# Short convolution, its silu, its product and its root moved to later picks of the gather loop

## The chip, the cores and the metric

The kernel runs on one core of one Trainium2 chip. The metric is the device time of one execution in microseconds (us), as the median of several runs; less is better. "PE" is the matrix engine, "DVE" the vector engine, "ACT" the scalar engine, "POOL" the GpSimd engine and "SP" the sync engine.

## The reference

One layer of a streaming encoder for 1024 frames of width 1024. First comes token mixing, then an expert layer in which every frame fetches 128 pairs of rows from two tables of 16384 experts:

```python
proj = jnp.einsum('bsd,dc->bsc', rms_norm(h, norm_mix_gain), w_in)
p_in, q_raw, k_raw, v_raw, z, b_raw, a_raw = jnp.split(proj, SPLIT_POINTS, axis=-1)
pool_out = multiscale_pool_mixer(p_in, w_pool, b_pool, pool_scale)
qkv = silu(causal_depthwise_conv(concat(q_raw, k_raw, v_raw), conv_w))   # 4 taps
q, k = l2_normalize(q) * HEAD_DIM ** -0.5, l2_normalize(k)
o = gated_delta_rule_chunked(q, k, v, g, beta)                            # 4 heads, chunks of 64
h = h + concat(pool_out, rms_norm(o, o_gain) * silu(z)) @ w_out
# expert layer, for blocks of 128 frames
q = h_t @ w_query                    # 8 heads x 2 halves
s1, s2 = q[:, :, 0] @ sub_keys_1, q[:, :, 1] @ sub_keys_2
experts, gates = top 16 of the sums of the two top 16's, softmax
act = gelu(h_t . expert_u[experts])
h = h + sum over (gates * act) * expert_v[experts]
out = rms_norm(h, norm_final_gain)
```

## The kernel before, in words

**The gather loop.** The frames are worked on in 8 tiles of 128. A tile has 8 retrieval heads with 16 picks each, so 128 picks, and the loop has 1024. At each pick POOL issues one indirect transfer (L806) that brings one row of both expert tables for each of the 128 frames, 1 MB, into one of 8 places of a ring. DVE multiplies and sums the row with the frame (L1504, "the dot"). ACT takes the gelu of the sum (L1107), scales a small diagonal with it (L1111) and makes the next diagonal (L1099). After every odd pick PE adds two picks with 16 matmuls (L1845 and L1846, "the pair"; in the last tile L1829). Only when the pair of an old pick is done may POOL issue the transfer that overwrites its place, eight picks later. In the text 3/3.7 is pick 7 of head 3 of tile 3, tiles, heads and picks being counted from 0.

**What else runs in the loop.** Everything else is laid beside the picks by a hand-written order. Each engine has its own loop over the picks and at each pick does the pick's own work first and then what is due: the search for the next heads' picks on DVE (`search`), the delta rule of the next tile as 35 steps for each of two pairs of heads (`delta`, begun at picks 13 and 45 of a tile, so that its steps 3 to 18 lie on heads 1 and 3), the scores of a later head on PE (L1760, picks 12 and 13), the norms. On ACT step 5 of the delta rule is the copy L926 and steps 6, 9, 12 and so on the copy L929; PE's products of these steps are L1537.

**The units.** The input projection of the later frames is cut into 38 units of 128 output columns by 256 frames, one unit in each head from 0/5 on. A unit w is worked on by the functions called `unit`, over two heads. In its own head PE projects it in two halves (L1691, 8 matmuls each in the trace), ACT copies it out of the accumulator at pick 11 (L1061 to L1065), and DVE makes the four taps of its convolution (L1439 and three times L1441) at picks 12 to 15. In the next head ACT takes the silu (L1039) and, for the query and key units, the square (L1042); PE sums the squares by one product (L1670); ACT takes the root (L1047); DVE makes the reciprocal (L1416) and the product (L1419) at picks 8 and 9; at pick 11 the result is stored. There are 16 query and key units ("q"), 8 value units ("v", no square and no root), 8 pooling units and 6 gate units. Whether the weights of a unit are loaded late is told by `load_late`.

**Order on an engine.** Instructions of an engine start in the order in which they stand. ACT does the pick (L1107, L1111, L1099), then `unit`, then `delta`; PE does `delta`, then the pair, then `unit`, then the scores; DVE does the dot, the search, `delta`, then `unit`.

## Time and profile before

| what | value |
|---|---|
| median of 3 runs | 2986.09 us (2985.65 to 2986.99) |
| the profiled execution, its own time | 2982.09 us |
| its span, first to last instruction | 2979.9 us |
| busy: PE, DVE, ACT, POOL | 78%, 73%, 50%, 42% |
| granted clock of PE, mean | 0.913 of 2.4 GHz |
| first and last gather issued | 258.6 us, 2953.4 us |

The profile is of one execution. Its own time is the span and 2.2 us around it. In the timelines each row has the start and the length of an instruction or of a few merged ones, and in brackets how long the engine had been idle before it and what it waited for. The length of a merged row goes from the start of the first to the end of the last.

### The profile page before, as it was taken

Reading aid. Unit: us, or ns where it says so; the run is one execution under the profiler, and the core shown is the slowest. Engines: PE = TensorE matmul, PEld = TensorE weight load, DVE = VectorE, ACT = ScalarE, POOL = GpSimd, SP = SyncE. Lnnn points to the kernel's source line nnn. Section 1 sums busy time; section 2 is a strip of 40 time slices with the busy share of each in tenths; the row PEclk is TensorE's granted clock in tenths of the full one; section 3 lists DMA queues with packets and bytes.
Section 4 is the critical chain, followed back from the end, with each engine's and each line's share of the span. In section 5 each row is a group of like instructions: output and inputs, shape, how many; then the busy total and the mean of one; then the engine's idle time right before and its main releaser. Section 6 shows DMA issues by size and latency. Waiting matters only on the chain.

```text
span 2979.9 us, 38619 instructions
## 1 busy us (share of the span) xinstructions
PE 2329.6 (78%) x12696; PEld 1126.5 (38%) x12696; DVE 2185.6 (73%) x5443; ACT 1484.0 (50%) x4204; POOL 1240.4 (42%) x1168
## 2 busy tenths in 40 slices
PE   7998778778886778677786778767786778778887
PEld 6454444234432444233442344324431333223332
DVE  2756776788877886778887887678876787776664
ACT  3623455565654554444655654544453454444444
POOL 1002444444444444443444344444444444544442
PEclk9999899889898999898998889889997888989999
DMA  4435999999999999999999999999999999999998
GB/s 169 151 112 220 408 419 413 421 421 407 408 420 421 418 418 419 419 416 408 404 420 421 407 420 415 420 418 419 404 415 421 418 411 415 404 416 420 421 421 345
DMA packets 194009, 1157.77 MB, mean 389 GB/s; under 512 B 20880, under 2 KB 48912, under 8 KB 62224
## 3 DMA queue, kind: packets, MB, share of 16 engines
q0 software_dynamic: 147456, 1073.81, 87.1%
q1 hardware_dynamic: 29392, 55.54, 5.2%
q10 hardware_dynamic: 16960, 25.96, 2.3%
q8 instruction: 101, 1.65, 0.2%
q14 instruction: 100, 0.82, 0.1%
HBM read 1139.49 MB, written 15.73 MB: 388 GB/s over the span
## 4 chain that ended last, share of the span: by engine, by line
DMA 41%; PE 26%; DVE 10%; ACT 9%; issue 4%; POOL 3%; ACTq 0%; DVEq 0%; POOLq 0%
DMA ring_mem<-in_experts,work 41%; PE bank L1845 11%; DVE ring_mem L1504 6%; POOL ring_mem L806 3%; PE bank L1713 3%; PE bank L1829 3%; PE bank L1537 3%; PE bank L1760 2%; ACT work L1111 2%; ACT L1107 1%; ACT work L1107 1%; ACT L984 1%; ACT work L1099 1%; PE bank L1691 1%; PE bank L1638 1%
## 5 line engine op out<-in xcount | busy, mean ns | idle before, releaser
L806 POOL DMA_INDIRECT ring_mem<-in_experts,work x1024 | 1174.9, 1147 | 1464.9 <-PE bank L1846 1145.8
L1504 DVE CUSTOM_DVE_ANT_0 ring_mem<-ring_mem,work 128x1024 f32<-128x1024 f32 x1024 | 1251.9, 1223 | 557.3 <-DMA ring_mem<-in_experts,work 553.4
L1845 PE MATMUL bank<-ring_mem,work 64*64 64x512 f32 x3584 | 1016.3, 687 | 356.5 <-ACT work L1111 356.3
L1846 PE MATMUL bank<-ring_mem,work 64*64 64x512 f32 x3584 | 1016.3, 687 | 0.0
L1107 ACT ACTIVATE work<-work 128x1 f32<-128x1 f32 x1024 | 206.0, 201 | 1197.3 <-DVE work L1504 1192.3
L1845 PEld LDWEIGHTS bank<-ring_mem,work 64*64 64x64 f32 x3584 | 247.8, 147 | 854.7 <-ACT work L1111 504.1
L1111 ACT ACTIVATE work<-work 128x64 f32<-128x64 f32 (+1 forms) x1024 | 364.0, 355 | 34.1 <-ACT work L1107 0.2
L1099 ACT ACTIVATE work<-kept,work 128x64 f32<-128x64 f32 x896 | 298.4, 333 | 10.9 <-DVE work L1377 10.9
L1829 PE MATMUL bank<-ring_mem,work 128*128 128x512 f32 x512 | 248.8, 621 | 47.1 <-ACT work L1111 46.7
L1537 PE MATMUL bank<-work 128*128 128x128 f32 x1080 | 190.5, 316 | 117.9 <-ACT work L929 54.9
L1760 PE MATMUL bank<-late,work 128*128 128x256 f32 x1008 | 253.9, 396 | 9.8 <-ACT late L964 7.5
L1537 PEld LDWEIGHTS bank<-work 128*128 128x128 f32 x1080 | 155.8, 213 | 249.9 <-ACT work L929 82.5
L1846 PEld LDWEIGHTS bank<-ring_mem,work 64*64 64x64 f32 x3584 | 248.0, 147 | 0.0
L1760 PEld LDWEIGHTS bank<-late,work 128*128 128x128 f32 x1008 | 188.4, 195 | 118.1 <-issue 88.5
L1107 ACT ACT_TABLE_LOAD x152 | 195.0, 1283 | 4.8 <-ACT ring_mem L1057 2.2
L1829 PEld LDWEIGHTS bank<-ring_mem,work 128*128 128x128 f32 x512 | 92.6, 194 | 196.4 <-ACT work L1111 117.0
L800 POOL COPY work<-work 128x8 int32<-128x8 int32 x128 | 56.0, 438 | 193.6 <-DVE work L1369 192.8
L1691 PE MATMUL bank<-ring_mem,work 128*128 128x256 f32 x512 | 128.5, 395 | 0.1
L1691 PEld LDWEIGHTS bank<-ring_mem,work 128*128 128x128 f32 x512 | 94.8, 195 | 45.5 <-issue 34.7
L1713 PE MATMUL bank<-x_all,work 128*128 128x512 f32 x224 | 105.3, 614 | 0.0
L440 PE MATMUL bank<-ring_mem,late 128*128 128x512 f32 x224 | 97.9, 593 | 1.5 <-PEq L217 1.5
L1504 DVE DVE_READ_ACCUMULATOR2_ANT work<- 128x1 f32 x1024 | 84.4, 82 | 0.0
(328 smaller groups left out, 2503.3 us busy)
## 6 DMA issues: line engine op xcount, KB each, us to landing
work<-in_wc ACTq DMA_DIRECT2D x37, 512.0 KB
ring_mem<-in_experts,work POOLq DMA_INDIRECT x1024, 12.7
ring_mem<-in_w_query SPq DMA_DIRECT2D x16, 576.0 KB, 7.7
late<-in_wc SPq DMA_DIRECT2D x16, 512.0 KB, 3.8
work<-kept_tiles SPq DMA_DIRECT2D x42, 128.0 KB, 7.9
x_all<-in_x SPq DMA_DIRECT2D x8, 512.0 KB, 12.5
x_all<-in_w_out SPq DMA_DIRECT2D x1, 4096.0 KB, 18.4
work<-in_x SPq DMA_DIRECT2D x8, 512.0 KB, 8.6
```

The source lines that it names most:

```text
L806: G.indirect_dma_start(ring[k % RING], None, a["experts"], bass.IndirectOffsetOnAxis(ap=pick_now[:, k:k + 1], axis=0)).then_inc(got[k % RI ...
L1099: A.activation(diag[k % DIAGS], pair_ident, ACT.Copy, scale=gates[:, ds(j * TOPK + k, 1)]).then_inc(X["weights_made"], 1)
L1107: A.activation(scored_gelu[:, k:k + 1], dots[:, k:k + 1], ACT.Gelu).then_inc(X["gelu_made"], 1)
L1111: A.activation(of, of, ACT.Copy, scale=scored_gelu[:, k:k + 1]).then_inc(X["diag_made"], 1)
L1504: V.tensor_tensor_reduce(out=row, in0=row, in1=hf_tile[t % 2], scale=1.0, scalar=0.0, op0=ALU.mult, op1=ALU.add, accum_out=dots[:, k:k + 1 ...
L1537: m = PE.matmul(to[:, c], left[:, c], right[:, c], start=True, stop=True)
L1691: p = PE.matmul(bank[2][:, 0:PW], weights_place(w)[:, d * P:(d + 1) * P], hn_now[:, d * PW:(d + 1) * PW], start=(d == 0), stop=(d == DB - 1))
L1713: m = PE.matmul(mixed_bank(t, half), hf_tile[t % 2][:, d * P:(d + 1) * P], w_out[:, d * DM + half * HALF:d * DM + (half + 1) * HALF], star ...
L1760: m = PE.matmul(bank[2][:, 0:QD], hf_t[:, d * P:(d + 1) * P], w_score[:, ds(j * QD + d * (PHEADS * QD), QD)], start=(d == 0), stop=(d == D ...
L1829: m = PE.matmul(low_sum[half], whole_diag[k % (DIAGS // 2)], ring[k % RING][:, DM + half * HALF:DM + (half + 1) * HALF], start=False, stop ...
L1845: PE.matmul(low_sum[half][high if odd else low], of[low], row[low], start=(q == 1 and odd == 1), stop=(q == PICKS - 1))
L1846: m = PE.matmul(high_sum[half][low if odd else high], of[high], row[high], start=(q == 1 and odd == 1), stop=(q == PICKS - 1))
```

## The change

The four taps of a unit's convolution move on DVE from picks 12 to 15 of the unit's own head to picks 0 to 3 of the next. The silu and the square move on ACT from pick 2 to pick 4, PE's product of the squares and its pooling product from pick 4 to 5, the root from pick 5 to 6, DVE's end of a pooling unit from pick 6 to 7. The projection's two halves, until now at picks 6 and 8 (8 and 9 where the weights are loaded late), stand at picks 8 and 9 in every head. DVE's reciprocal and product at picks 8 and 9, ACT's copies, loads and stores at pick 11, the pooling sums at picks 12 to 15 and the late load at pick 2 stay.

```diff
         def project_at(w):
-            return (8, 9) if w >= GROWN or load_late(w) else (6, 8)
+            return 8, 9
...
-                    if k == 2 and 0 <= m < GROWN and i < Z_UNIT:
+                    if k == 2 and 0 <= m < GROWN and 12 <= i < Z_UNIT:
                         act.wait_ge(U["summed"], sums(w))
+                    if k == 4 and 0 <= m < GROWN and i < Z_UNIT:
                         if i < 12:
+                            act.wait_ge(U["summed"], sums(w))
                             if m > 0:
                                 act.wait_ge(U["stored"], 16 * m)
                             A.activation(unit_now[:, 0:PW], sum_now[:, PAD:], ACT.Silu).then_inc(U["silu_made"], 1)
...
-                    if k == 5 and 0 <= m < GROWN and i < 8:
+                    if k == 6 and 0 <= m < GROWN and i < 8:
                         act.wait_ge(U["second"], seconds(w))
...
-                    if 0 <= m < GROWN and 12 <= i < Z_UNIT and k == 6:
+                    if 0 <= m < GROWN and 12 <= i < Z_UNIT and k == 7:
...
-                    if w >= GROWN or k < 12 or now >= Z_UNIT:
+                    if k < TAPS and 0 <= m < GROWN and i < 12:
+                        if k == 0:
+                            dve.wait_ge(U["raw_kept"], m + 1)
+                            if m > 0:
+                                dve.wait_ge(U["done"], seconds(m))
+                                dve.wait_ge(U["silu_made"], silus(m))
+                        else:
+                            vc.settle()
+                        dst = sum_now[:, PAD:]
+                        tap = small[:, 4 * i + TAPS - 1 - k:4 * i + TAPS - k]
+                        if k == 0:
+                            vc.mark(V.tensor_scalar(dst, raw_now[:, PAD:], tap, None, ALU.mult))
+                        else:
+                            s = V.scalar_tensor_tensor(dst, raw_now[:, PAD - k:PAD + PW - k], tap, dst, ALU.mult, ALU.add)
+                            if k < TAPS - 1:
+                                vc.mark(s)
+                            else:
+                                s.then_inc(U["summed"], 1)
+                    if w >= GROWN or k < 12 or not 12 <= now < Z_UNIT:
                         return
...
-                    if k == 4 and 0 <= m < GROWN and (i < 8 or 12 <= i < Z_UNIT):
+                    if k == 5 and 0 <= m < GROWN and (i < 8 or 12 <= i < Z_UNIT):
                         pe.wait_ge(X["scores_read"], window(w) + AHEAD + 1)
```

The three places below are in head 1/3, where both the convolution and the delta rule are due. Line numbers of the changed kernel are 2 higher on DVE and ACT for the same work (8 higher for the dot and on PE).

On ACT, before, picks 2 and 3: the copy L926 of the delta rule's step 5 stands behind the silu L1039 and the square L1042.

```order
L1107 ACTIVATE work<-work 128x1
L1111 ACTIVATE work<-work 128x64
L1099 ACTIVATE work<-kept,work 128x64
L1039 ACT_TABLE_LOAD
L1039 ACTIVATE ring_mem<-ring_mem 128x256
L1042 ACTIVATE ring_mem<-ring_mem 128x256
L926 ACTIVATE work<-bank 128x256
L1107 ACT_TABLE_LOAD
L1107 ACTIVATE work<-work 128x1
L1111 ACTIVATE work<-work 128x64
L1099 ACTIVATE work<-kept,work 128x64
L929 ACTIVATE work<-bank 128x256
```

On ACT, the changed kernel, from the end of pick 2 to the start of pick 5: the silu is L1041 and the square L1044.

```order
L926 ACTIVATE work<-bank 128x256
L1109 ACTIVATE work<-work 128x1
L1113 ACTIVATE work<-work 128x64
L1101 ACTIVATE work<-kept,work 128x64
L929 ACTIVATE work<-bank 128x256
L1109 ACTIVATE work<-work 128x1
L1113 ACTIVATE work<-work 128x64
L1101 ACTIVATE work<-kept,work 128x64
L1041 ACT_TABLE_LOAD
L1041 ACTIVATE ring_mem<-ring_mem 128x256
L1044 ACTIVATE ring_mem<-ring_mem 128x256
L1109 ACT_TABLE_LOAD
```

The two table loads, the silu and the square have moved behind L926, pick 3, L929 and pick 4.

On DVE, picks 1 and 2 before: dot, search, then the delta rule.

```order
L1504 ISA ring_mem,work<-ring_mem,work 128x1024
L1504 ISA work 128x1
L1315 MATCH_REPLACE work<-work,bank 128x128
L1316 MAX_INDEX work<-work,bank 128x8
L1207 COPY work<-work 128x4
L1209 SCALAR_TENSOR_TENSOR work<-work 128x256
L1210 SCALAR_TENSOR_TENSOR work<-bank,work 128x256
```

On DVE, the same pick in the changed kernel, with what stands before the next dot.

```order
L1512 ISA ring_mem,work<-ring_mem,work 128x1024
L1512 ISA work 128x1
L1317 MATCH_REPLACE work<-work,bank 128x128
L1318 MAX_INDEX work<-work,bank 128x8
L1209 COPY work<-work 128x4
L1211 SCALAR_TENSOR_TENSOR work<-work 128x256
L1212 SCALAR_TENSOR_TENSOR work<-bank,work 128x256
L1440 SCALAR_TENSOR_TENSOR ring_mem<-ring_mem 128x256
```

One tap, L1440, now stands at the end of the pick; picks 0, 2 and 3 end with one as well, and those at picks 12 to 15 are gone.

On PE, before, the last two matmuls of the pair of picks 8 and 9 (L1845, L1846), step 14 of the delta rule (L1537) and the first two of the next pair.

```order
L1845 MATMUL bank<-ring_mem,work 64x512
L1846 MATMUL bank<-ring_mem,work 64x512
L1537 MATMUL bank<-work 128x128 x2
L1845 MATMUL bank<-ring_mem,work 64x512
L1846 MATMUL bank<-ring_mem,work 64x512
```

On PE, the same place in the changed kernel.

```order
L1853 MATMUL bank<-ring_mem,work 64x512
L1854 MATMUL bank<-ring_mem,work 64x512
L1699 MATMUL bank<-ring_mem,work 128x256 x4
L1545 MATMUL bank<-work 128x128 x2
L1853 MATMUL bank<-ring_mem,work 64x512
L1854 MATMUL bank<-ring_mem,work 64x512
```

The second half of the projection (L1699, the L1691 of before) stands between the two pairs; the half that stood before the pair of picks 6 and 7 is gone from there.

## Rows read from the trace of the kernel before

**Rows 1.** The page: GB/s in 40 slices, and the group of the dot.

```profile
GB/s 169 151 112 220 408 419 413 421 421 407 408 420 421 418 418 419 419 416 408 404 420 421 407 420 415 420 418 419 404 415 421 418 411 415 404 416 420 421 421 345
...
L1504 DVE CUSTOM_DVE_ANT_0 ring_mem<-ring_mem,work 128x1024 f32<-128x1024 f32 x1024 | 1251.9, 1223 | 557.3 <-DMA ring_mem<-in_experts,work 553.4
```

**Rows 2.** Windows, heads 1/3, 3/3, 4/0, 4/1, 2/4: busy per engine, clock, DMA, GB/s.

```profile
743.10:786.10 43.00, 34.12 (x224) 18.62 (x224) 38.27 (x99) 26.37 (x72) 20.62 (x19) 0.92 0.98 400
1429.50:1472.30 42.80, 34.01 (x224) 18.52 (x223) 38.42 (x99) 26.21 (x71) 19.91 (x18) 0.92 0.96 392
1642.60:1685.20 42.60, 32.60 (x206) 15.65 (x202) 35.85 (x88) 28.50 (x71) 20.34 (x18) 0.92 1.00 407
1685.20:1728.10 42.90, 34.84 (x212) 18.22 (x204) 38.60 (x99) 26.00 (x71) 19.06 (x18) 0.84 1.00 411
1126.10:1169.80 43.70, 35.25 (x225) 17.36 (x226) 31.02 (x81) 23.17 (x67) 18.49 (x19) 0.96 1.02 419
```

**Rows 3.** POOL's timeline in head 1/3: start, length, engine, line; idle before.

```profile
762.26 0.93 POOL L806 DMA_INDIRECT ring_mem<-in_experts,work  x1 [8.27 <-PE bank L1846]
```

**Rows 4.** PE's timeline in head 1/3: steps 5 and 6, a pair, a product.

```profile
754.17 0.68 PE L1537 MATMUL bank<-work 128*128 128x128 f32 x4 [3.25 <-ACT work L926]
...
756.49 2.08 PE L1537 MATMUL bank<-work 128*128 128x128 f32 x8 [1.63 <-ACT work L929]
758.50 1.11 PE L1845 MATMUL bank<-ring_mem,work 64*64 64x512 f32 x1
...
761.91 0.70 PE L1670 MATMUL bank<-ring_mem,work 128*128 128x256 f32 x2
```

**Rows 5.** ACT's timeline in head 1/3, pieces of picks 2, 3 and 5.

```profile
750.75 0.20 ACT L1107 ACTIVATE work<-work 128x1 f32<-128x1 f32 x1 [1.59 <-DVE work L1504]
...
751.60 1.28 ACT L1039 ACT_TABLE_LOAD   x1
752.89 0.42 ACT L1039 ACTIVATE ring_mem<-ring_mem 128x256 f32<-128x256 f32 x1
...
753.66 0.37 ACT L926 ACTIVATE work<-bank 128x256 f32<-128x256 f32 x1
...
756.07 0.36 ACT L929 ACTIVATE work<-bank 128x256 f32<-128x256 f32 x1
...
762.65 0.47 ACT L1047 ACTIVATE ring_mem<-bank,eps_col 128x256 f32<-128x256 f32 x1 [3.49 <-PE bank L1670]
```

**Rows 6.** PE's timeline in head 2/3: steps 5 and 6 with no silu.

```profile
1093.69 0.68 PE L1537 MATMUL bank<-work 128*128 128x128 f32 x4 [1.06 <-ACT work L926]
1096.08 2.04 PE L1537 MATMUL bank<-work 128*128 128x128 f32 x8 [1.70 <-ACT work L929]
```

**Rows 7.** Groups by line: the second to fourth tap on DVE.

```profile
L1441 DVE SCALAR_TENSOR_TENSOR ring_mem<-ring_mem 128x256 f32<-128x256 f32 x72 | 34.7, 483 | 1.8
```

**Rows 8.** Head 4/0: the dot of pick 3, and the square sum behind pick 3.

```profile
1652.31 1.21 DVE L1504 CUSTOM_DVE_ANT_0 ring_mem<-ring_mem,work 128x1024 f32<-128x1024 f32 x1
...
1657.25 1.04 ACT L998 ACTIVATE work<-work 128x1024 f32<-128x1024 f32 x1
```

**Rows 9.** PE's timeline in head 4/0: first matmul of three pairs.

```profile
1657.16 0.64 PE L1845 MATMUL bank<-ring_mem,work 64*64 64x512 f32 x1 [2.66 <-ACT work L1111]
...
1659.67 0.64 PE L1845 MATMUL bank<-ring_mem,work 64*64 64x512 f32 x1
...
1664.26 0.64 PE L1845 MATMUL bank<-ring_mem,work 64*64 64x512 f32 x1 [0.60 <-ACT work L1111]
```

**Rows 10.** Line L806, issue to landing: the whole run, then the window of 3/6.

```profile
DMA to landing us min/median/max: 5.9/12.7/18.3
DMA to landing us min/median/max: 10.4/13.3/15.3
```

**Rows 11.** PE's timeline in head 1/3: the second half, and step 14.

```profile
770.82 1.89 PE L1691 MATMUL bank<-ring_mem,work 128*128 128x256 f32 x8
...
776.38 0.71 PE L1537 MATMUL bank<-work 128*128 128x128 f32 x4
```

More of the change, by code:

```diff
@@ L1434, in unit @@
                         vc.settle()
-                    if now < 12:
-                        dst = sum_now[:, PAD:]
-                        tap = small[:, 4 * now + TAPS - 1 - step:4 * now + TAPS - step]
-                        if step == 0:
-                            vc.mark(V.tensor_scalar(dst, raw_now[:, PAD:], tap, None, ALU.mult))
-                        else:
-                            m = V.scalar_tensor_tensor(dst, raw_now[:, PAD - step:PAD + PW - step], tap, dst, ALU.mult, ALU.add)
-                            if step < TAPS - 1:
-                                vc.mark(m)
-                            else:
-                                m.then_inc(U["summed"], 1)
-                        return
                     first_of_tile = window(w) % PHEADS == 0
```

## The prediction

> **What bounds the kernel now.** I read four views. The page first: from the fifth slice to the last but one the traffic is 404 to 421 GB/s, and what the dot waits for is the gather, 553.4 of its 557.3 us of idle time [rows 1]. So the loop runs at the pace of the DMA engines. A change of order can only give back time in which they fall short of their rate, or add such time; PE at 78% and DVE at 73% busy are not the limit. Then the windows by head. A head without a burst of unit work on ACT at pick 2 moves 419 GB/s (2/4). Head 1/3 moves 400 (1/1 has the same figure), 3/3 392, 4/0 407, 4/1 411 (and 4/3 the same) [rows 2]. All six have a query, key or value unit in its second head, and five of them also have steps 3 to 18 of the delta rule. At 420 GB/s the shortfalls are 43.0 x 20/420 = 2.0 us for 1/3, 2.0 for 1/1, 42.8 x 28/420 = 2.9 for 3/3, 42.6 x 13/420 = 1.3 for 4/0, and 42.9 x 9/420 = 0.9 each for 4/1 and 4/3. Together that is 10.0 us. I know of no other place that the change touches and that falls short of the rate.
>
> Third, the timelines of 1/3, to see what makes the shortfall. POOL stands idle for 8.27 us until the pair of picks 2 and 3 is done, and issues at 762.26 [rows 3]. That pair starts at 758.50, behind step 6 of the delta rule; step 6 waited 1.63 us for ACT's L929, and step 5 before it waited 3.25 us for ACT's L926 [rows 4]. L926 stands behind the table load that begins at 751.60, the silu and the square, and starts at 753.66; the load for the next gelu, of the same length, pushes the rest [rows 5]. PE meanwhile has dropped: step 6 takes 2.08 us and the pair's first matmul 1.11, where a matmul of this kind takes 0.64 [rows 4, 9]; the granted clock of the windows of the short heads is 0.84 to 0.92, in 2/4 it is 0.96 [rows 2]. Fourth, the time from issue to landing: 12.7 us as a median, 5.9 at the least [rows 10]. What lies above about 6 is queue, that is, the delay that a late pair can have before the DMA engines run dry.
>
> **The change part by part.** No instruction is added or removed, nor any byte; DVE's, ACT's and PE's sums stay, and SP's and POOL's order too. Table loads are as many as before: silu and root are still each alone between two gelus.
>
> *Silu and square off pick 2, in heads with the delta rule (1/1, 1/3, 3/3, 4/1 for q, 4/3 for v).* Without the burst L926 could start at 751.60 instead of 753.66, 2.06 us earlier. Against it stand the taps: those at picks 0 and 1 lie ahead of the dot of pick 2, 2 x 0.48 [rows 7] = 0.97 us. L926 and with it step 5 come 2.06 - 0.97 = 1.1 us earlier, at 753.1. Step 6 started 2.39 us after step 5 in 2/3, where no silu is in the way [rows 6]; the tap at pick 2 adds 0.48. So step 6 starts at 753.1 + 2.9 = 756.0, 0.5 us earlier than 756.49, and so does the pair. That is the low end. The high end is that PE does not drop: 2/3 shows step 6 at 2.04 us although the gaps were only 1.06 and 1.70 us [rows 6], so step 6 stays slow, but the pair behind it may run fast in part; the pair took 761.91 - 758.50 = 3.4 us [rows 4]; by the ratio of 0.64 to 1.11 for its first matmul [rows 9, 4] it takes about 2.0 at the high level, 1.4 to 1.5 less. The range is 0.5 to 2.0 us per head, and I take 1.2, since the idle time of PE ahead of step 5 shrinks by a third. No head can give more than its shortfall: 1.2 x 3 for 1/1, 1/3 and 3/3, and 0.8 each for 4/1 and 4/3: 5.2 us.
>
> At this place the Trainium skill has a price, in "ScalarE: Activation LUTs", section "What ACT_TABLE_LOAD costs": a switch of set costs 1283 ns and a drain of about 1380 ns more. The trace disagrees on the second: the load at 751.60 ends at 752.88 and the silu starts at 752.89 [rows 5]. By the page's 2.66 us each of the burst's two switches would be 1.38 us dearer, and both the relief at pick 2 and the delay at pick 4 would grow by that; the measurement decides, and my sum uses 1.28.
>
> *The same in head 4/0 (and 1/0 and 2/0, which are not short).* The pair of picks 2 and 3 started at 1657.16 after 2.66 us of waiting for the diagonal [rows 9]. Now the dot of pick 3 starts at 1652.31 + 3 x 0.48 = 1653.8 [rows 7, 8], and with 1.22 for the dot and 0.6 for gelu and diagonal the pair starts at 1655.6, 1.5 us earlier. Capped by the shortfall of 1.3 and with part of it lost again below, I take 0.8.
>
> *The burst at pick 4 and the root at pick 6.* Before, the root stood behind an odd pick, so the pair was released ahead of it. Now both bursts stand behind even picks and delay the second pick of a pair. In 4/0: pick 3 done 1655.9, the square sum of the norm 1.04 [rows 8] to 1657.0, pick 4 0.85 (750.75 to 751.60 in [rows 5]) to 1657.8, load, silu and square 2.1 to 1659.9, load 1.28 and diagonal 0.6 to 1661.8. The pair of 4 and 5 started at 1659.67 [rows 9]: 2.1 us later. It takes 2.0, the product 0.70 [rows 4] to 1664.5, the root 0.47 with its load hidden in the wait [rows 5], load and diagonal 1.9 to 1666.9. The pair of 6 and 7 started at 1664.26: 2.6 us later. In the q heads with neither norm nor delta rule the queue covers that: 3/6 has 10.4 us at the least against 5.9 [rows 10], 4.5 us of cover, and nothing is lost. In heads 1/1, 1/3, 3/3 and 4/1 PE itself was late there: its product stood at 761.91 [rows 4] and the root waited 3.49 us for it [rows 5], so the burst at pick 4 falls into a wait, and the half projection of 1.89 us that stood ahead of the pair of 6 and 7 is gone. I put the pair of 6 and 7 there at no change. Bounds over all: 0 (covered everywhere) to 2.6 us in each of the two q heads at the start of a tile (1/0, 4/0): 5 us. I take 1.0.
>
> *The second half behind the pair of 8 and 9.* 26 units had their halves at 6 and 8. In 1/3 the second half ended at 772.71 and step 14 began at 776.38 straight behind the pair [rows 11]; from there PE has no idle time to the end of the head. So the 1.89 us now put behind the pair make the pairs of 10 to 15 that much later. The queue at these picks is not shown apart; by the median of 12.7 against 5.9 us it covers far more than 1.9 [rows 10]. Bounds: 0, and 1.9 us less 0.6 for idle time ahead in each of four heads, 5 us. I take 1.0. ACT's copies at pick 11 wait for this half; behind them stands the gelu of pick 12, whose pair waits for the same PE anyway.
>
> *Taps off picks 12 to 15; product and pooling output one pick later; DVE's new waits.* The waits are for things finished at pick 11 or 9 of the head before. DVE has 1.9 us less at the end of a head, where the gather and not DVE was late. Nothing; bounds -1 to +1.
>
> Sum: -5.2 - 0.8 + 1.0 + 1.0 = -4.0 us on the profiled execution's 2982.09 (span 2979.9 and 2.2 around it). The median of the runs before is 2986.09, 4.0 above that execution; the same step from it gives 2982.1.
>
> **The rivals.**
> *A, full relief:* DMA engines stay fed in all six heads, -10.0 us: 2976. For it speaks that the queue needs only 1 to 2 us more and that a head without the burst moved 419; against it that step 6 remains slow in 2/3 and that the taps lag DVE at picks 1 to 4. Chance 0.25.
> *B, slower:* the bursts at picks 4 and 6 form one chain, silu, pair, product, root, pair, and PE drops in the wait of over 3 us that now stands ahead of the pair of 4 and 5. The pair then takes 3.4 instead of 2.0 us and the pair of 6 and 7 comes 2.6 + 1.5 = 4.1 us late in all 16 q heads. It decides where the landing time at these picks is under 5.9 + 4.1 = 10.0 us: in the heads at starts of tiles and those with the delta rule, 6 heads, at about 2.5 us each, 15 us, less 5 of relief: +10, 2996. Against it: in the four delta heads the root waited for PE before, too. Chance 0.17.
> *C, nothing moves:* the taps eat what the silu gives back, and the shortfall stays: within 1.5 us, 2986. The low end of 0.5 us per head speaks for it. Chance 0.15. That the order doesn't change as said is excluded by the order shown.
> *The forecast,* -2 to -6: chance 0.43.
>
> **How the numbers follow.** What a measurement of this kernel can tell from no change is taken as 0.2%, 6.0 us. Faster than that: A and a twentieth beyond the forecast's edge, 0.29. Slower: B, 0.17. Between: the rest of the forecast and C, 0.54. The range takes in A's end with some room for PE's clock and half of B: 2972 to 2993; 0.1 is left below, 0.1 above. The predicted time is 2982.1.
>
> **What would show it.** In 1/3 and 3/3: step 5 of the delta rule starts about 1 us earlier after the dot of pick 2, step 6 0.5 us, the gather behind the pair of 2 and 3 is issued 1 to 2 us sooner, the windows rise from 400 and 392 to about 412 GB/s. In 4/0 the pairs of 4 and 5 and of 6 and 7 start 2 to 2.6 us later than before, counted from their dots, with no loss of GB/s. DVE's dots of picks 2 to 5 lag the landings by up to 2 us more. I am wrong if 3/3 stays under 400 GB/s, if a q head that moved 420 falls under 412, or if new short windows appear at picks 14 and 15.

## The result, and the profile after

| kernel | median, us | range, us | runs |
|---|---|---|---|
| before | 2986.22 | 2981.28 to 2993.17 | 21 |
| changed | 2994.48 | 2989.41 to 3004.53 | 21 |

The ratio is 1.0032, 95% interval 1.0024 to 1.0039: slower by 0.32%, some 9.5 us (the two medians are 8.3 apart). The forecast was 2982.1 and its range ended at 2993; the time lies on the side of rival B.

The profiled execution of the changed kernel took 2996.69 us; its span of 2994.7 is 14.8 above that of before. By the starts of the dots this splits into 4.6 us ahead of head 0/5 (the first dot comes at 273.5 and not 269.7; of the kernels below, which change nothing there either, two show 269.7 and the others 272.2 to 274.5), 8.0 in heads 0/5 to 5/3, where the units are, and 2.2 behind them, where nothing is changed. The page, in the lines that answer to [rows 1], and the groups of the gather and of the pair:

```profile
GB/s 164 154 110 204 410 416 409 421 400 418 409 419 421 417 419 419 419 415 414 397 402 421 403 413 416 419 420 417 406 401 421 411 410 414 406 416 420 421 421 347
L806 POOL DMA_INDIRECT ring_mem<-in_experts,work x1024 | 1169.4, 1142 | 1479.7 <-PE bank L1854 1163.3
L1512 DVE CUSTOM_DVE_ANT_0 ring_mem<-ring_mem,work 128x1024 f32<-128x1024 f32 x1024 | 1251.5, 1222 | 543.6 <-DMA ring_mem<-in_experts,work 532.6
L1853 PE MATMUL bank<-ring_mem,work 64*64 64x512 f32 x3584 | 1034.5, 699 | 379.6 <-ACT work L1113 374.3
```

Slices 9, 20 and 21 are lower, 400, 397 and 402 where there were 421, 404 and 420. POOL waits 18 us longer for the pairs (1145.8 before) and the pairs 18 us longer for the diagonal (356.3). The dot waits 21 us less for its gather. The taps between the dots of picks 0 to 3 don't explain that by themselves: with root at 7, below, they stand there too, and the dot waits 553.6 us. POOL's longer wait says that the DMA engines are asked later. The windows of heads 1/3, 3/3, 4/0 and 4/1, as [rows 2], and of 3/5:

```profile
749.54:791.78 42.24, 33.06 (x216) 17.32 (x215) 38.17 (x99) 27.02 (x73) 19.80 (x18) 0.92 1.00 400
1436.09:1479.91 43.82, 35.18 (x222) 18.94 (x222) 38.28 (x100) 26.87 (x72) 20.79 (x19) 0.88 0.98 387
1651.47:1696.89 45.42, 33.55 (x186) 15.70 (x181) 35.89 (x87) 29.50 (x72) 18.02 (x18) 0.81 0.99 400
1696.89:1739.45 42.56, 32.95 (x215) 17.40 (x214) 38.28 (x100) 25.14 (x69) 18.54 (x18) 0.92 0.98 401
1522.11:1567.16 45.05, 39.53 (x226) 18.03 (x218) 32.58 (x81) 27.06 (x69) 19.26 (x18) 0.96 0.97 394
```

3/3 stays under 400 GB/s, and 3/5, a q head that moved 420, is down at 394: two of the three signs that the prediction named against itself. 1/3 was to rise to about 412 GB/s and stays at 400. 4/0 is 2.8 us longer, and it shows the third sign, a short window at picks 14 and 15, here before and then changed:

```profile
1678.19:1685.17 6.98, 6.74 (x48) 4.32 (x51) 5.54 (x13) 2.11 (x7) 3.09 (x3) 1.00 1.01 418
```

```profile
1690.05:1696.89 6.84, 6.84 (x42) 4.84 (x41) 4.67 (x11) 3.30 (x10) 4.32 (x4) 1.00 0.98 379
```

**The relief at pick 2 came.** In 1/3 the dot of pick 2 starts at 757.52. PE's steps 5 and 6 of the delta rule, as [rows 4], and the gather behind the pair of picks 2 and 3, as [rows 3]:

```profile
760.02 0.68 PE L1545 MATMUL bank<-work 128*128 128x128 f32 x4
...
762.80 1.88 PE L1545 MATMUL bank<-work 128*128 128x128 f32 x8 [2.10 <-ACT work L929]
```

```profile
767.73 0.93 POOL L806 DMA_INDIRECT ring_mem<-in_experts,work  x1 [4.04 <-PE bank L1854]
```

From that dot to step 5 it is 2.5 us, before 4.7 (754.17 less 749.50, that kernel's dot of pick 2); to the gather it is 10.2, before 12.8. More relief than the 1.2 us that I took.

**The delay behind it came too, and was larger.** Head 4/0 on ACT, from the silu of pick 4 to the diagonal of pick 7:

```profile
1664.51 1.28 ACT L1041 ACT_TABLE_LOAD   x1
...
1666.69 1.28 ACT L1109 ACT_TABLE_LOAD   x1
...
1668.21 0.35 ACT L1113 ACTIVATE work<-work 128x64 f32<-128x64 f32 x1
...
1669.53 1.28 ACT L1049 ACT_TABLE_LOAD   x1
1673.50 0.47 ACT L1049 ACTIVATE ring_mem<-bank,eps_col 128x256 f32<-128x256 f32 x1 [2.68 <-PE bank L1678]
1673.99 1.28 ACT L1109 ACT_TABLE_LOAD   x1
...
1675.52 0.35 ACT L1113 ACTIVATE work<-work 128x64 f32<-128x64 f32 x1
```

And on PE: the pair of 4 and 5, the product, the pairs of 6 and 7 and of 8 and 9:

```profile
1668.62 1.11 PE L1853 MATMUL bank<-ring_mem,work 64*64 64x512 f32 x1 [4.44 <-ACT work L1113]
...
1672.24 1.22 PE L1678 MATMUL bank<-ring_mem,work 128*128 128x256 f32 x2
1675.92 1.11 PE L1853 MATMUL bank<-ring_mem,work 64*64 64x512 f32 x1 [2.46 <-ACT work L1113]
...
1684.06 0.64 PE L1853 MATMUL bank<-ring_mem,work 64*64 64x512 f32 x1
```

PE waits 4.44 us, its clock has dropped to the lower level (1.11 for the first matmul against 0.64 in [rows 9]), the pair takes 3.7 us, the product behind it 1.22, and the root, whose table has long been loaded, stands 2.68 us in front of the diagonal of pick 7. What POOL sees of it: the gathers behind the pairs of 6 and 7 and of 8 and 9, in the kernel before:

```profile
1666.48 1.54 POOL L806 DMA_INDIRECT ring_mem<-in_experts,work  x1 [1.99 <-PE bank L1846]
...
1672.57 0.96 POOL L806 DMA_INDIRECT ring_mem<-in_experts,work  x1 [1.40 <-PE bank L1846]
```

and in the changed one:

```profile
1679.88 1.50 POOL L806 DMA_INDIRECT ring_mem<-in_experts,work  x1 [5.12 <-PE bank L1854]
...
1686.78 1.16 POOL L806 DMA_INDIRECT ring_mem<-in_experts,work  x1 [3.96 <-PE bank L1854]
```

Counted from the dot of pick 4 (1653.98 and 1662.41) they are issued 5.0 and 5.8 us later. Of the first 5.0 us, 3.2 are the later start of the pair of 6 and 7 (13.5 us after that dot, before 10.3), and 1.7 are its length, 3.7 us instead of 2.0.

Over the run, the root's wait on ACT in 16 heads, and that of the first of ACT's copies at pick 11:

```profile
L1049 ACT ACTIVATE ring_mem<-bank,eps_col x16: 473/473/474, 554.5 to 1718.3; 128x256 f32<-128x256 f32 x16
its engine sat idle before it (us, times) until:
  PE bank L1678: 22.1, 14
```

```profile
its engine sat idle before it (us, times) until:
  PE bank L1699: 36.7, 19
```

Before, the same two views give 14.6 us in 6 waits and 8.4 us in 6.

### The profile page after: what moved, and what is told of

It reads as the page before. It is cut to its first block, busy times and chain, and to the rows that moved or that the text cites. A ratio compares the mean times of both kernels' runs of the same rounds, so it can differ in the third digit from the quotient of the medians.

```text
span 2994.7 us, 38619 instructions
## 1 busy us (share of the span) xinstructions
PE 2340.0 (78%) x12696; PEld 1124.9 (38%) x12696; DVE 2180.6 (73%) x5443; ACT 1484.7 (50%) x4204; POOL 1236.7 (41%) x1168
## 4 chain that ended last, share of the span: by engine, by line
DMA 36%; PE 31%; DVE 11%; ACT 8%; issue 4%; POOL 3%; another core or an unknown queue 0%; ACTq 0%; DVEq 0%; POOLq 0%
DMA ring_mem<-in_experts,work 36%; PE bank L1853 14%; DVE ring_mem L1512 6%; PE bank L1721 3%; POOL ring_mem L806 3%; PE bank L1768 3%; PE bank L1837 2%; PE bank L1545 2%; PE bank L1699 2%; ACT work L1113 1%; ACT L1109 1%; ACT work L1109 1%; ACT L984 1%; PE bank L1652 1%; ACT work L1101 1%
## 5 line engine op out<-in xcount | busy, mean ns | idle before, releaser
L806 POOL DMA_INDIRECT ring_mem<-in_experts,work x1024 | 1169.4, 1142 | 1479.7 <-PE bank L1854 1163.3
L1853 PE MATMUL bank<-ring_mem,work 64*64 64x512 f32 x3584 | 1034.5, 699 | 379.6 <-ACT work L1113 374.3
L1854 PE MATMUL bank<-ring_mem,work 64*64 64x512 f32 x3584 | 1034.6, 699 | 0.0
L1853 PEld LDWEIGHTS bank<-ring_mem,work 64*64 64x64 f32 x3584 | 251.9, 148 | 884.6 <-ACT work L1113 520.5
L1545 PE MATMUL bank<-work 128*128 128x128 f32 x1080 | 183.4, 308 | 104.2 <-ACT work L929 58.1
L1768 PE MATMUL bank<-late,work 128*128 128x256 f32 x1008 | 251.0, 393 | 10.7 <-ACT late L964 8.6
L1854 PEld LDWEIGHTS bank<-ring_mem,work 64*64 64x64 f32 x3584 | 252.0, 148 | 0.0
L1699 PE MATMUL bank<-ring_mem,work 128*128 128x256 f32 x512 | 130.6, 399 | 0.0
L1699 PEld LDWEIGHTS bank<-ring_mem,work 128*128 128x128 f32 x512 | 95.4, 197 | 59.6 <-issue 48.6
## 6 DMA issues: line engine op xcount, KB each, us to landing
x_all<-in_x SPq DMA_DIRECT2D x8, 512.0 KB, 12.5
```

Of the source, the lines that this page charges most:

```text
L806: G.indirect_dma_start(ring[k % RING], None, a["experts"], bass.IndirectOffsetOnAxis(ap=pick_now[:, k:k + 1], axis=0)).then_inc(got[k % RI ...
L1545: m = PE.matmul(to[:, c], left[:, c], right[:, c], start=True, stop=True)
L1699: p = PE.matmul(bank[2][:, 0:PW], weights_place(w)[:, d * P:(d + 1) * P], hn_now[:, d * PW:(d + 1) * PW], start=(d == 0), stop=(d == DB - 1))
L1768: m = PE.matmul(bank[2][:, 0:QD], hf_t[:, d * P:(d + 1) * P], w_score[:, ds(j * QD + d * (PHEADS * QD), QD)], start=(d == 0), stop=(d == D ...
L1853: PE.matmul(low_sum[half][high if odd else low], of[low], row[low], start=(q == 1 and odd == 1), stop=(q == PICKS - 1))
L1854: m = PE.matmul(high_sum[half][low if odd else high], of[high], row[high], start=(q == 1 and odd == 1), stop=(q == PICKS - 1))
```

## The experiments

Each was compared with the kernel before on the same chip, in five rounds. Ratios have their 95% intervals. "Pick 10's flight" is the time from POOL's issue of the gather of pick 10 to its last landing, as the mean of the five delta heads of the prediction (1/1, 1/3, 3/3, 4/1, 4/3); "pick 14's flight" is that of pick 14 in the other 19 of the 24 heads in which a silu stands. Pick 14's gather stands behind the pair of 6 and 7, pick 10's behind that of 2 and 3. A long flight is read here as queue, and the queue as the reserve; the shortest flight of all before was 5.9 us [rows 10]. "Pair of 6 and 7" is the mean length of that pair in the 16 heads with a root, from the start of its first matmul to the end of its last; it takes 1.95 us at PE's higher clock and up to 3.7 at the lower. All of this is of one profiled execution each.

| kernel | ratio | root waits, us | copies at 11 wait, us | pick 14's flight | pick 10's flight | pair of 6 and 7, us |
|---|---|---|---|---|---|---|
| before | 1 | 14.6 | 8.4 | 13.4 | 6.7 | 1.95 |
| changed | 1.0032 (1.0024 to 1.0039) | 22.1 | 36.7 | 10.2 | 7.2 | 2.69 |
| projection only | 1.0012 (1.0004 to 1.0021) | 15.5 | 25.9 | 12.6 | 6.2 | 2.03 |
| bursts only | 1.0000 (0.9991 to 1.0009) | 23.2 | 7.8 | 11.4 | 10.4 | 1.95 |
| bursts, product at 4 | 1.0001 (0.9992 to 1.0010) | 0 | 9.2 | 11.6 | 9.8 | 1.95 |
| taps back | 1.0009 (0.9999 to 1.0018) | 23.6 | 37.1 | 10.6 | 8.1 | 2.74 |
| projection back | 1.0011 (1.0001 to 1.0020) | 21.3 | 8.0 | 11.0 | 7.6 | 1.95 |
| root at 7 | 1.0002 (0.9993 to 1.0011) | 4.9 | 31.0 | 12.5 | 7.6 | 2.04 |
| root at 7, taps back | 1.0003 (0.9994 to 1.0012) | 4.6 | 35.0 | 12.3 | 9.8 | 2.06 |
| product at 4 | 1.0006 (0.9997 to 1.0015) | 0 | 26.3 | 12.5 | 8.0 | 2.22 |
| product at 4, root cut | 1.0034 (1.0022 to 1.0046) | 0 | 35.1 | 10.7 | 7.6 | 2.82 |
| before, root cut | 1.0003 (0.9994 to 1.0012) | 15.7 | 7.9 | 12.7 | 6.6 | 2.13 |
| bursts at 3 and 5 | 1.0033 (1.0020 to 1.0046) | 8.4 | 21.0 | 12.6 | 6.2 | 2.59 |
| silu at 5, root at 7 | 1.0005 (0.9995 to 1.0015) | 0 | 30.4 | 12.8 | 7.6 | 2.21 |

Neither the flights nor the pair orders the ratios by itself. A flight of 12.6 us for pick 14 goes with 1.0012 and with 1.0033, 10.6 with 1.0009 and 10.7 with 1.0034, and 11.4 with no loss. The pair of 6 and 7 is at 2.6 to 2.8 us in the three kernels at 1.0032 to 1.0034, and in taps back, which is at 1.0009.

**Projection only.** The kernel before with

```diff
-            return (8, 9) if w >= GROWN or load_late(w) else (6, 8)
+            return 8, 9
```

> The kernel before with one part of the change: both halves of the projection at picks 8 and 9 in every head; taps, silu, product and root stay. Theory 1 (the burst on ACT behind picks 4 and 6 and PE's clock behind it make the loss, the later half adds little): within 3 us of before, ratio 0.999 to 1.001. Theory 2 (the second half behind the pair of picks 8 and 9, and ACT's copies at pick 11 that wait for it, make most of the loss): 6 to 10 us slower, ratio 1.002 to 1.003.

1.0012: between the two. What grew is a wait that I had argued away. The first copy at pick 11 on ACT and, behind it, the first tap on DVE at pick 12:

```profile
its engine sat idle before it (us, times) until:
  PE bank L1691: 25.9, 15
```

```profile
its engine sat idle before it (us, times) until:
  ACT ring_mem L1065: 5.6, 5
```

Behind the copies stands the gelu of pick 12, behind the tap the dot of pick 13.

**Taps back.** The changed kernel with its four taps at picks 12 to 15 of the unit's own head:

```diff
-                    if k < TAPS and 0 <= m < GROWN and i < 12:
...
-                    if w >= GROWN or k < 12 or not 12 <= now < Z_UNIT:
+                    if w >= GROWN or k < 12 or now >= Z_UNIT:
...
+                    if now < 12:
...
```

> The changed kernel with the four taps back at picks 12 to 15 of the unit's own head; silu at 4, product at 5, root at 6 and projection at 8 and 9 as changed. Theory 1 (ACT's chain silu, pair, product, root, pair makes the loss): still 6 to 10 us slower than before, ratio 1.002 to 1.003. Theory 3 (the taps at picks 0 to 3 delay the dots, and that is the loss): within 3 us of before.

1.0009, inside theory 3's range, although the root waits as long as in the changed kernel. Theory 1, as I had it, missed: the root's wait is not a cost by itself.

**Bursts at odd picks.** Silu at 3, product 4, root 5, pooling output 6.

```diff
-                    if k == 4 and 0 <= m < GROWN and i < Z_UNIT:
+                    if k == 3 and 0 <= m < GROWN and i < Z_UNIT:
...
-                    if k == 6 and 0 <= m < GROWN and i < 8:
+                    if k == 5 and 0 <= m < GROWN and i < 8:
```

> The changed kernel with silu and square at pick 3, product at 4 and root at 5 (both bursts on ACT behind odd picks, where the pair has its diagonal already); taps at 0 to 3 and projection at 8 and 9 as changed. Theory 1: most of the loss is gone, 0 to 3 us above before, ratio 0.999 to 1.001, and in the heads at the start of a tile the pair of picks 6 and 7 is not over 1 us later than before. Theory 2 and theory 3: no better than the changed kernel, 6 to 10 us slower.

1.0033: missed. In the delta heads a silu behind pick 3 stands in front of the copy L929, on which step 6 and the pair of 2 and 3 wait. Step 6 in 1/3, and the windows of 1/1, 1/3 and 3/3:

```profile
764.18 2.08 PE L1545 MATMUL bank<-work 128*128 128x128 f32 x8 [4.23 <-ACT work L929]
```

```profile
658.98:705.23 46.25, 35.11 (x207) 18.37 (x200) 38.12 (x100) 25.63 (x71) 17.99 (x18) 0.82 0.97 385
749.65:793.23 43.58, 33.42 (x213) 17.08 (x213) 38.13 (x99) 26.22 (x71) 16.07 (x16) 0.88 0.94 378
1437.97:1482.62 44.65, 34.03 (x215) 17.99 (x215) 38.18 (x99) 26.08 (x70) 16.81 (x18) 0.85 0.93 375
```

Before, those heads moved 400, 400 and 392. An odd pick is not enough: it also matters what the burst stands in front of.

**Root at 7.**

```diff
-                    if k == 6 and 0 <= m < GROWN and i < 8:
+                    if k == 7 and 0 <= m < GROWN and i < 8:
```

> The changed kernel with the root at pick 7 instead of 6: ACT no longer waits for PE's product between the two picks of a pair, all else as changed. Theory 1: half or more of the loss goes, since the pair of 6 and 7 is not held by the wait and the two table loads; 1 to 5 us slower than before, ratio 1.000 to 1.0015. Theory 2 and theory 3: 6 to 10 us slower as the changed kernel.

1.0002, a hit for theory 1: one number taken back returns nearly the whole loss. But theory 3 was a hit in taps back, so the two costs cannot simply add. This kernel also differs in more than the wait. In 1/0, 4/0, 1/5 and 3/5 a small square root of a norm stands behind pick 7 (L1002, L1011), and the two roots now share one table load: the kernel makes 320 table loads, and the changed one and the one before 328. The same holds for the other two kernels with the root at 7. 4/0 and 3/5 are the heads that grew most in the changed kernel.

**Bursts only.** The kernel before with the bursts at 4 and 6 and the products at 5 (output of pooling units at 7); taps and projection stay.

```diff
-                    if k == 2 and 0 <= m < GROWN and i < Z_UNIT:
+                    if k == 4 and 0 <= m < GROWN and i < Z_UNIT:
...
-                    if k == 5 and 0 <= m < GROWN and i < 8:
+                    if k == 6 and 0 <= m < GROWN and i < 8:
...
-                    if k == 4 and 0 <= m < GROWN and (i < 8 or 12 <= i < Z_UNIT):
+                    if k == 5 and 0 <= m < GROWN and (i < 8 or 12 <= i < Z_UNIT):
```

> The kernel before with silu and square at pick 4, product at 5 and root at 6, the projection at 6 and 8 and the taps at 12 to 15 as before. The run with taps put back (bursts and projection moved) came to 1.0009. Theory 1 (the root at an even pick waits for the product behind the pair, and each pair from 4 to 9 comes later by that): the fault is all here, but the half projection at pick 6 also waits for the root and stands ahead of the pair of 6 and 7: 1.001 to 1.003, and in 0/7 and 3/6 the pair of 6 and 7 is at least 5 us late. Rival 2 (the halves of the projection at 8 and 9 carry the 0.1% of that run, the bursts cost nothing net): 0.998 to 1.0005.

1.0000: rival 2. In 0/7 and 3/6 the pair of 6 and 7 starts 3.6 us later, counted from the dot of pick 4, and not the 5 of theory 1. The run shows two things. The root's wait is here too, 23.2 us in 14 waits, and the kernel is no slower (without it, below, 1.0001):

```profile
L1049 ACT ACTIVATE ring_mem<-bank,eps_col x16: 474/474/475, 554.5 to 1708.8; 128x256 f32<-128x256 f32 x16
its engine sat idle before it (us, times) until:
  PE bank L1672: 23.2, 14
```

And the rate after the relief at pick 2, in 1/1, 1/3, 3/3, 4/1 and 4/3:

```profile
659.42:701.32 41.90, 32.14 (x216) 16.77 (x208) 38.32 (x99) 25.86 (x72) 21.62 (x19) 0.96 1.01 421
745.30:787.54 42.24, 33.47 (x224) 18.32 (x223) 38.32 (x100) 26.64 (x72) 19.65 (x19) 0.96 1.02 419
1433.27:1475.50 42.23, 34.86 (x223) 18.09 (x221) 38.36 (x99) 26.29 (x71) 20.86 (x19) 0.92 1.01 412
1689.57:1731.90 42.33, 32.16 (x216) 16.93 (x208) 38.30 (x100) 26.19 (x71) 21.38 (x18) 0.96 1.01 421
1775.85:1817.89 42.04, 33.62 (x227) 18.57 (x226) 36.78 (x97) 23.17 (x67) 22.06 (x19) 0.96 1.01 421
```

400, 392 and 411 GB/s have become 412 to 421, yet the five heads are only 3.0 us shorter together (210.7 against 213.8 us), and the kernel is no faster.

**Root at 7 and taps back.** The edits of these two kernels together, `k == 7` for the root and the taps under `if now < 12`.

> The changed kernel with the root at pick 7 and the taps back at picks 12 to 15. Root at 7 alone gave 1.0002, taps back alone 1.0009. Theory 1 (two separate costs, root 0.3% and taps up to 0.2%): both gone, 0.998 to 0.9995, the relief at pick 2 shows in the time. Rival 3 (both take from one reserve, the queue of the DMA engines at picks 12 to 15, so that either remedy is enough): 0.9995 to 1.001, no better than root at 7 alone. The flight of pick 14's gather from issue to landing in 3/6 tells how much reserve there is: 8.3 us in the changed kernel, 13.0 with root at 7.

1.0003: rival 3, with the interval (0.9994 to 1.0012) just reaching theory 1's range. The second remedy adds nothing measurable to the first. That the queue is what both take from, the second half of rival 3, this ratio can't show.

**Product at 4.** The root stays at 6; PE's product stands ahead of the pair of 4 and 5.

```diff
-                    if k == 5 and 0 <= m < GROWN and (i < 8 or 12 <= i < Z_UNIT):
+                    if 0 <= m < GROWN and ((k == 4 and i < 8) or (k == 5 and 12 <= i < Z_UNIT)):
```

> The changed kernel with PE's product of the squares put back to pick 4, that is ahead of the pair of 4 and 5 and not behind it; the root stays at pick 6, the pooling product at 5. Theory 1 (the root's wait for the product behind the slow pair is the cost; in 4/0 it was 2.7 us): the root no longer waits, 0.999 to 1.0015. Rival 4 (the root behind an even pick costs by itself, its two table loads delay the diagonal of pick 7 whether or not it waits): 1.0025 to 1.004. The delay of the diagonal of pick 7 from its dot in 4/0 was 6.9 us in the changed kernel, 4.2 before; theory 1 expects about 4.5.

1.0006: theory 1. In 4/0 the root, the product and the pair of 6 and 7:

```profile
1667.23 0.47 ACT L1049 ACTIVATE ring_mem<-bank,eps_col 128x256 f32<-128x256 f32 x1
```

```profile
1663.22 0.67 PE L1678 MATMUL bank<-ring_mem,work 128*128 128x256 f32 x2 [2.63 <-ACT ring_mem L1044]
...
1669.66 1.11 PE L1853 MATMUL bank<-ring_mem,work 64*64 64x512 f32 x1 [1.48 <-ACT work L1113]
```

The product lies in PE's wait, and the root starts with its table. The diagonal of pick 7 ends 4.7 us after the start of its dot (expected 4.5, in the changed kernel 6.9). In this head the pair of 6 and 7 still runs at the lower clock, but over the 16 heads it takes 2.22 us as a mean and not 2.69: the run takes away part of the low clock together with the wait.

**Silu at 5, root at 7.** As root at 7, with silu and square at pick 5 and both products at 6.

```diff
-                    if k == 4 and 0 <= m < GROWN and i < Z_UNIT:
+                    if k == 5 and 0 <= m < GROWN and i < Z_UNIT:
...
-                    if k == 5 and 0 <= m < GROWN and (i < 8 or 12 <= i < Z_UNIT):
+                    if k == 6 and 0 <= m < GROWN and (i < 8 or 12 <= i < Z_UNIT):
```

> The changed kernel with silu and square at pick 5, both products of PE at 6, the root at 7: every burst behind an odd pick, taps at 0 to 3, projection at 8 and 9. Theory 1 (a burst costs where it holds the diagonal a pair waits for, and behind an odd pick it does not): as root at 7 or better, 0.998 to 1.0005. Rival 5 (as in the run with bursts at 3 and 5, 1.0033: a burst ahead of a copy of the delta rule delays that rule and with it the pairs, wherever it stands): 1.001 to 1.004, with heads 1/1, 1/3, 3/3 and 4/3 longer by 1 to 3 us each.

1.0005, against 1.0033 with the bursts at 3 and 5: at the edge of theory 1, and no better than root at 7. Of the four heads of rival 5, 1/1 and 3/3 are 1.6 and 1.2 us longer, 1/3 is 1.4 shorter and 4/3 unchanged.

**Projection back.** The changed kernel with only the projection's halves at 6 and 8 again.

```diff
-            return 8, 9
+            return (8, 9) if w >= GROWN or load_late(w) else (6, 8)
```

> The changed kernel with the projection's halves back at picks 6 and 8 (8 and 9 for late loads); taps at 0 to 3, silu at 4, product at 5, root at 6. Taps back came to 1.0009, taps and projection back to 1.0000. Theory R (root's wait, taps and late half draw on one reserve, the queue of the DMA engines at picks 8 to 15; any one of them given back is nearly enough): 0.9995 to 1.0015. Rival S (root's wait is the whole fault and the others only chance to hide it): still 1.002 to 1.0035, since the root waits here as in the changed kernel.

1.0011: in theory R's range, with an interval that ends where rival S begins. A third remedy returns two thirds of the loss, with the root's wait still at 21.3 us. It does touch the root's chain in one way: a half projection stands ahead of the pair of 6 and 7 again, and the pair takes 1.95 us in this kernel where it took 2.69.

**Bursts, product at 4.** Bursts only, with the product of the squares at pick 4 as before.

```diff
-                    if k == 5 and 0 <= m < GROWN and (i < 8 or 12 <= i < Z_UNIT):
+                    if 0 <= m < GROWN and ((k == 4 and i < 8) or (k == 5 and 12 <= i < Z_UNIT)):
```

> The kernel before with only silu and square moved to pick 4 and the root to pick 6; product at 4, projection at 6 and 8, taps at 12 to 15: the relief at pick 2 with none of the three costs. Theory R: 0.998 to 0.9995, faster than both kernels by 2 to 6 us, with the flight of pick 10's gather in the five heads with the delta rule at 9 to 10 us (6.7 before). Rival C (DMA engines that run dry at pick 10 are made good within the head, nothing to be gained): 0.9997 to 1.0005.

1.0001: rival C, though the interval (0.9992 to 1.0010) leaves room for up to 2.4 us of gain. The version to which the experiments point doesn't measurably beat the kernel before.

**Product at 4, root cut.** The wait that went is replaced by work:

```diff
-                        A.activation(sum_now[:, PAD:], bank[2][:, PW:], ACT.Sqrt, bias=eps_col).then_inc(U["root_made"], 1)
+                        for c in range(0, PW, 32):
+                            s = A.activation(sum_now[:, PAD + c:PAD + c + 32], bank[2][:, PW + c:PW + c + 32], ACT.Sqrt, bias=eps_col)
+                        s.then_inc(U["root_made"], 1)
```

> The run with the product at pick 4 (1.0006), and its root, which no longer waits, cut into 8 pieces of 32 columns: about 2 us more of ACT work behind pick 6, as long as the wait that went (22 us in 14 waits, 1.6 us each). Theory R (what costs is that the diagonal of pick 7 comes late, whatever the reason): the loss is back, 1.002 to 1.004, and the diagonal of pick 7 is again late by 1 to 2 us. Rival O (what had cost is PE's order, the product between the pair of 4 and 5 and the next pair): 1.0005 to 1.0015.

```profile
L1050 ACT ACTIVATE ring_mem<-bank,eps_col x128: 278/301/332, 551.6 to 1719.0; 128x32 f32<-128x32 f32 x128
```

```profile
1674.14 1.53 ACT L1050 ACTIVATE ring_mem<-bank,eps_col 128x32 f32<-128x32 f32 x8
```

The first row is the source line over the run, the second ACT's timeline in 4/0. The pieces overlap: eight of 0.30 us take 1.53 from the first start to the last end, 1.1 us more than the one of 0.47, not the 2 that I had expected. Even so the loss is back, 1.0034 against 1.0006: theory R. The diagonal of pick 7 ends 5.3 us after the start of its dot as the mean of the 16 heads, against 4.1 without the cut, 1.2 later. The pair of 6 and 7 is also slow again, 2.82 us against 2.22.

**Before, root cut.** The same cut in the kernel before, behind pick 5.

> The kernel before with the same cut of the root, behind pick 5 and ahead of no diagonal that a pair waits for alone, 2 us more of ACT work in the same 16 heads. Theory R (a delay costs only where the reserve has been used by something else; here the flight of pick 14's gather is 13.4 us, in the changed kernel 10.2): 0.9998 to 1.001. Rival W (2 us more on ACT in 16 heads cost wherever they are): 1.002 to 1.004.

1.0003, in theory R's range. The same 1.1 us of ACT work in the same 16 heads costs nothing measurable here and 0.28% there. This doesn't yet show that the other moves make the difference, since the place differs as well: here the cut stands behind pick 5, and makes the diagonal of pick 7 0.9 us later and not 1.2. The cut in the kernel with only the bursts moved would separate the two, and wasn't run. Behind an odd pick, with the pair released and taps and projection elsewhere, it takes 0.7 us off pick 14's flight (13.4 to 12.7); behind pick 6 of the changed order it takes 1.8 (12.5 to 10.7).

## Why the prediction was wrong

**What the runs show.** The moves don't add up. The clearest case is the root's wait, which the product at pick 4 takes away. In the changed kernel that gives back 0.26%, and with bursts only nothing (1.0001 without the wait, 1.0000 with it), each to about 0.12 either way. Yet the wait makes the diagonal of pick 7 equally late in both: as the mean of the 16 heads with a root it ends 5.6 us after the start of its dot against 4.1 without the wait in the changed order, and 5.0 against 3.5 with bursts only. With the root at 7, the taps or the projection taken back the loss falls from 0.32% to 0.02, 0.09 and 0.11%. These three remedies, 0.30, 0.23 and 0.21%, come to 0.74% together, over twice the loss. For the taps and the projection apart from the root the numbers don't tell more than a plain sum: projection only and projection back make 0.12 + 0.11 = 0.23%, against 0.32, to about 0.15 either way.

**What stays open** is what the moves share. I read it as one reserve, the queue of the DMA engines: all three delay the issue of gathers behind picks 4 to 12, and pick 14's flight falls from 11.4 to 6.4 us in 4/0 and from 13.4 to 6.4 in 1/0. No run shows that this is the whole of it, and the mean flights don't order the ratios. A rival is PE's clock: the pair of 6 and 7 lasts 2.6 to 2.8 us in the three slowest kernels and 1.95 to 2.2 in all the others but taps back, and in every kernel with a half projection at pick 6, ahead of this pair, and the bursts late, it took 1.95. Taps back, 2.74 us and 1.0009, speaks against the clock alone. No run changes the one without the other.

*The part that failed: the burst at pick 4 and the root at pick 6, +1.0 us, and the cover given to it.* The step was 2.1 us later for the pair of 4 and 5 and "2.6 us later" for the pair of 6 and 7, at 2.0 us a pair. Counted from the dot of pick 4, in 4/0 the two pairs start 0.5 and 3.2 us later, so the starts were not what went wrong; but each takes 3.7 us, and the gather behind the second comes 5.0 later. I had put PE's drop of clock in rival B alone, though a wait of 4.2 us in front of the pair followed from my own times (1655.6 and 2.0 for the pair before, 1661.8 for this one). The second half of the step, "nothing is lost" because the queue covers it, was worked out for this term alone, and so for the projection: the same cover was counted for each edit by itself. With the bursts moved alone the root's wait did cost nothing; beside the other two moves it is worth 0.26%, 8 us.

*The second half of the projection, +1.0 us.* Alone it is +0.12%, 3.6 us (1.2 to 6.3), inside my bounds of 0 to 5, and mis-sized. The sentence that excused ACT's copies was wrong: their wait went from 8.4 to 25.9 us in that run and to 36.7 in the changed kernel, and the diagonal of pick 12 stands behind them.

*The taps, 0 with bounds of -1 to +1.* Beside the other edits they are worth 0.23% (0.32 less 0.09), 7 us; with the projection at its old place 0.11%, which the intervals don't tell from nothing. I counted DVE's time and its waits, and not what four later dots do beside the bursts.

*The relief at pick 2, -6.0 us.* The mechanism was right and larger than forecast: 2.6 us at the gather in 1/3. Its price is the largest miss of the sum. I had taken GB/s missing in a window as time to be won, 10 us in six heads. With bursts only the five delta heads move 412 to 421 GB/s and are 3.0 us shorter, and the kernel is the same within 0.09%. That run has the relief and the bursts' own cost in it: the two terms, -6.0 and +1.0 in my sum, came to between -2.7 and +2.7 us, and without the root's wait to the same (1.0001). How that splits no run shows, nor why full rate in those heads buys no more; the other 19 heads gave back 2.0 us in that profile (814.6 against 812.6).

*Rival B* had the sign, the chain and the clock right; it expected the loss in six heads, the starts of tiles and the delta heads. The heads that grew most are 4/0 (+2.8), 3/5 (+1.8), 4/2 (+1.5), 3/6 (+1.3), 0/6 (+1.2) and 3/3 (+1.0); 1/3 (-0.8) and 4/1 (-0.4) became shorter. And it took the chain alone to be enough, against which speaks taps back: the whole chain with its slow pairs, and 1.0009. The chain is in heads with neither norm nor delta rule as well (the root waits 2.55 us in 3/6), which I had written off as covered.

*Against the Trainium skill:* the trace after agrees with the trace before on the table switch that I weighed ("ScalarE: Activation LUTs", section "What ACT_TABLE_LOAD costs"). The load takes 1.28 us and the silu starts 0.02 us after its end (1664.51, 1665.81), without the drain that the page adds.

## What to carry to other kernels

Cost the edits of one change together, and not each against the same slack: before giving a term "hidden", ask whether another term has been hidden behind the same thing. A wait that cost nothing alone was worth 0.26% here beside two other moves. And a missing GB/s in a window isn't a microsecond won: five heads were brought to 412 to 421 GB/s here for nothing measurable.

Before reading a remedy as the removal of one thing, count what else it changes. Root at 7 took away a wait and eight table loads; product at 4 gave the cleaner comparison.

When an operation is moved next to the one that feeds it on another engine, look at what now stands between the two in the feeder's queue: here the product stood behind a whole pair, and the waiting root in front of a diagonal.

## What the runs showed of the hardware

- In 4/0 of the changed kernel PE's granted clock was at the lower of its two levels after 4.44 us of waiting, for the whole pair, 3.7 us instead of 2.0, and for the product behind it, 1.22 us instead of 0.70. The next pair, behind a wait of 2.46 us, ran at the lower level too. In the same head of the kernel before, a pair behind a wait of 2.66 us ran at the higher level ([rows 9]).
- A square root and the small square root of a norm that stood next to each other on ACT took one table load: 320 loads with the root at pick 7, 328 with it at 6.
- Small activations of one kind on ACT overlap: a square root of 128x256 took 0.47 us, eight of 128x32 took 0.30 each and 1.53 together, not 2.4.
- The table load for the root is issued and done while ACT waits for its operand: the load at 1669.53 ended 2.68 us ahead of the root.
